# Norm of x in pairs of tiles, the first weight load moved up, and the second column tile three chunks behind in the first projection

## What is computed

```python
mod = einsum('bd,de->be', silu(cvec), w_ada) + b_ada        # 6 vectors of 1024, for two request groups
sh1, sc1, gt1, sh2, sc2, gt2 = split(mod, 6)
h    = rms_norm(x, norm1_g) * (1 + sc1) + sh1
proj = h @ w_in                                             # -> q | k | v | pool input xp | gate a | gate b
pool = multiscale_pool(xp, ...)                             # windows 2/4/8/16 over the tokens
```

## Time and profile before

| | us |
|---|---|
| median of three runs | 1836.32 |
| lowest, highest | 1834.43, 1836.9 |
| the profiled execution | 1835.91 |
| its span | 1834.0 |

### The profile page before, as it was taken

The page is one execution under the profiler, slowest core; times in us unless marked ns, Lnnn a source line. Parts: engine busy times, 40 slices in busy tenths (PEclk is TensorE's granted clock), DMA queues, the critical chain, the costliest instruction groups (busy, mean ns, idle before and its releaser), DMA issues. The chain is left out here.

```text
span 1834.0 us, 22375 instructions
## 1 busy us (share of the span) xinstructions
PE 1615.8 (88%) x8410; PEld 1279.4 (70%) x8410; DVE 905.8 (49%) x1226; ACT 603.4 (33%) x776; POOL 417.8 (23%) x232
## 2 busy tenths in 40 slices
PE   4999999999999699999999899989976599999910
PEld 3778888878887466666666588878865488888810
DVE  5650000006665666667666543331167566666559
ACT  5211121232222444444444500121122255555432
POOL 1111111112222400000000211121135234444353
PEclk9999999999999899999999999999988699999965
DMA  8223434230100600000000232231031378878555
GB/s 346 87 92 135 153 122 151 111 118 23 46 23 15 238 1 0 0 1 1 0 0 0 76 152 91 80 115 60 23 138 79 108 281 276 295 274 291 193 198 180
DMA packets 37888, 209.59 MB, mean 114 GB/s; under 512 B 4304, under 2 KB 5072, under 8 KB 27472
## 3 DMA queue, kind: packets, MB, share of 16 engines
q1 hardware_dynamic: 30352, 181.68, 26.8%
q0 software_dynamic: 7488, 27.27, 4.6%
HBM read 168.03 MB, written 49.28 MB: 118 GB/s over the span
## 5 line engine op out<-in xcount | busy, mean ns | idle before, releaser
L321 PE MATMUL psum<-h_hi,w_hi 128*128 128x512 f32 (+1 forms) x768 | 199.2, 368 | 12.8 <-DVE h_lo L619 7.8
L321 PE MATMUL psum<-h_lo,w_hi 128*128 128x512 f32 (+1 forms) x768 | 193.3, 360 | 0.0
L321 PE MATMUL psum<-h_hi,w_lo 128*128 128x512 f32 (+1 forms) x768 | 192.8, 359 | 0.0
L893 PE MATMUL psum<-probT,vals 128*128 128x512 f32 x384 | 190.9, 593 | 0.0
L954 ACT ACTIVATE prob<-psum,nmax 128x1536 f32<-128x1536 f32 x64 | 98.7, 1542 | 209.1 <-DVE nmax L1032 209.1
L321 PEld LDWEIGHTS psum<-h_hi,w_hi 128*128 128x128 f32 x768 | 128.4, 190 | 42.8 <-issue 22.5
L534 POOL TENSOR_TENSOR w_lo<-w_raw,w_hi 128x1024 fp32r<-128x1024 f32 x32 | 77.2, 2414 | 352.1 <-ACT w_hi L446 352.0
L909 PEld LDWEIGHTS psum<-ident,prob 128*128 128x128 f32 x768 | 92.9, 141 | 78.6 <-issue 72.6
L321 PEld LDWEIGHTS psum<-h_hi,w_lo 128*128 128x128 f32 x768 | 128.5, 189 | 23.0
L1029 DVE TENSOR_REDUCE rmax<-psum 128x1 f32<-128x512 f32 x192 | 128.9, 689 | 31.5 <-PE psum L885 31.4
L321 PEld LDWEIGHTS psum<-h_lo,w_hi 128*128 128x128 f32 x768 | 128.4, 189 | 23.0
(11 more groups left out here) (319 smaller groups left out, 3063.0 us busy)
## 6 DMA issues: line engine op xcount, KB each, us to landing
gu_raw<-in_w_gu SPq DMA_DIRECT2D x16, 2048.0 KB, 10.0
ada<-in_w_ada SPq DMA_DIRECT2D x20, 1024.0 KB, 4.8
w_raw<-in_w_in SPq DMA_DIRECT2D x16, 1024.0 KB, 4.8
dn_raw<-in_w_dn SPq DMA_DIRECT2D x16, 1024.0 KB, 8.3
ybuf<-yst SPq DMA_DIRECT2D x32, 512.0 KB, 7.5
gates<-gst SPq DMA_DIRECT2D x16, 640.0 KB, 3.0
wm_raw<-in_w_merge SPq DMA_DIRECT2D x4, 1536.0 KB, 6.9
xt<-in_x SPq DMA_DIRECT2D x10, 512.0 KB, 7.7
```

The lines of the kernel that those rows point to most:

```text
L321: mm = pe.matmul(psum[:, par_sets[j] + g:par_sets[j] + g + w], a[j][:, k, :], b[:, k, g:g + w], start=(k == 0 and a is w_hi and b is h_hi) ...
L893: mm = pe.matmul(psum[:, PV + 512 * x.par:PV + 512 * x.par + 512], vals[:, x.key0 // P + c, x.kv * HD:(x.kv + 1) * HD], probT[b][g % 2][:] ...
```

## The change

It has six parts.

1. The root and the reciprocals are made for two tiles at a time instead of five. ACT's copies of the transposed tiles stand between its squares (two tiles behind), DVE's stand two tiles behind its scaling.
2. PE turns all ten tiles first and does conditioning blocks 0 and 1 after them, each with its turn at once. In the chunk loop, block k+2 stands ahead of chunk k and its turn behind it, for k below 6. So six blocks and six turns lie in the loop, where four blocks and five turns did.
3. The second column tile runs three chunks behind the first (`LAG`), and its last three chunks follow the loop.
4. DVE modulates two chunks, then makes two `low`, then handles two conditioning blocks.
5. The first `w_raw` is loaded ahead of the conditioning blocks.
6. For the pool input, ACT splits the next weights ahead of its copies to `xpad`, and DVE raises `ada_rows1` and `mods_r1` ahead of the pooling.

```diff
+        LAG = 3
@@ sync
+                sp.dma_start(w_raw[:], io["w_in"][0]).then_inc(s["w_in0"], 16)
                 for i, b in enumerate(FIRST):
                     if i >= 6:
                         sp.wait_ge(s["fa_mm"], i - 5)
                     sp.dma_start(ada_first_buf[i][:], io["w_ada"][b]).then_inc(ada_first[i], 16)
-                    if i == 2:
-                        sp.dma_start(w_raw[:], io["w_in"][0]).then_inc(s["w_in0"], 16)
@@ tensor
-                for t in range(HALF):
+                for t in range(TILES):
                     turn_x(t)
                 pe.wait_ge(s["c_silu"], 1)
-                first_ada(0)
-                turn_x(HALF)
-                first_turn(0)
-                first_ada(1)
...
-                turn_x(HALF + 4)
-                first_ada(3)
+                for i in range(2):
+                    first_ada(i)
+                    first_turn(i)
...
                 for k in range(KC):
+                    if k < 6:
+                        first_ada(k + 2)
                     pe.wait_ge(s["h_hi_r"], k + 1)
                     pe.wait_ge(s["h_lo_r"], k + 1)
                     mm = project_k(0, k)
                     if k == KC - 1:
                         mm.then_inc(s["mm0"], 1)
-                    if k < 4:
-                        first_turn(k + 3)
-                        first_ada(k + 4)
-                    if k == 4:
-                        first_turn(7)
+                    if k < 6:
+                        first_turn(k + 2)
+                    if k >= LAG:
+                        project_k(1, k - LAG)
+                for k in range(KC - LAG, KC):
                     mm = project_k(1, k)
                 mm.then_inc(s["mm1"], 1)
@@ scalar
-                    if t % HALF == HALF - 1:
+                    if t % 2:
                         act.wait_ge(s["x_ss"], t + 1)
-                        h = slice(t + 1 - HALF, t + 1)
+                        h = slice(t - 1, t + 1)
                         nc.scalar.activation(rstd[:, h], ssq[:, h], ACT.Sqrt, bias=eps[:], scale=1.0 / D).then_inc(s["x_sq"], 1)
-                for t in range(TILES):
-                    act_out(t)
+                        if t > 2:
+                            act_out(t - 3)
+                            act_out(t - 2)
+                act_out(TILES - 2)
+                act_out(TILES - 1)
...
                 for n in range(XP_PAIRS):
                     for j in range(2):
+                        split(n + 1, j)
                         act.wait_ge(s[f"mm{j}"], n + 1)
...
                         act.sem_inc(s[f"ps_free{j}"], 1)
-                        split(n + 1, j)
@@ vector
+                for t in range(0, TILES, 2):
+                    h = slice(t, t + 2)
+                    dve.wait_ge(s["x_sq"], t // 2 + 1)
+                    own.step(nc.vector.tensor_scalar(nsq[:, h], ssq[:, h], 1.0 / D, EPS, ALU.mult, ALU.add))
+                    inverse(rstd[:, h], nsq[:, h], ntmp[:, h])
+                    for u in (t, t + 1):
+                        nc.vector.tensor_scalar(xt[:, u, :], xt[:, u, :], rstd[:, u:u + 1], None, ALU.mult).then_inc(s["x_scaled"], 1)
+                        if t:
+                            dve_out(u - 2)
+                dve_out(TILES - 2)
                 dve_out(TILES - 1)
+                for i in range(2):
+                    first_rows(i)
+                    first_mods(i)
...
-                modulate(0)
-                first_rows(3)
-                modulate(1)
-                low(0)
-                first_mods(3)
-                low(1)
-                for k in range(2, KC):
+                for k in range(0, KC, 2):
                     modulate(k)
                     if k < 6:
                         first_rows(k + 2)
+                    modulate(k + 1)
                     low(k)
+                    low(k + 1)
                     if k < 6:
                         first_mods(k + 2)
+                        first_rows(k + 3)
+                        first_mods(k + 3)
...
                 dve.wait_ge(s["h_lo_r"], KC)
+                dve.sem_inc(s["ada_rows1"], 1)
+                dve.sem_inc(s["mods_r1"], 1)
                 for c in range(4):
...
-                dve.sem_inc(s["ada_rows1"], 1)
-                dve.sem_inc(s["mods_r1"], 1)
```

## The result

The changed kernel took 1840.19 us (median of 14 runs, 1837.23 to 1842.25), the one before 1835.76 in the same comparison (14 runs, 1834.4 to 1837.58). The ratio is 1.0022, with a 95% interval of 1.0014 to 1.0029: slower by 4.4 us. The profiled execution took 1839.78 us with a span of 1837.9, 3.9 more than the span before.

What follows compares the result with a forecast made beforehand. TensorE, busy 88%, bounds the kernel; only its idles and low clock in the first 135 us could give. First chunk +2.0, loop +15.8 and pool input -12.3 sum to +5.5, so 1841.4 us; range 1833.5 to 1846.0.

Steps and rivals of the forecast that it cites:

- Part 6 and the gaps: Pool input: TensorE's gaps at 84.24 and 127.52 us close with their slow clock, gaining 5.2 and 7.1, together -12.3 us.
- The norm: Opening stage: all of x turned between 31 and 35.5 us, 33.5 taken; before it was 34.6.
- The first chunk: Start of the chunk loop: first chunk at about 45.3 us against 43.34, +2.0; ends 42.3 and 47.
- The hold by GpSimd: Ahead of the first chunk: POOL's two `w_lo` collide with DVE and hold `modulate(0)` by about 1.5 us.
- The loop: Chunk loop: 46 us with idles plus 7.1 of slow clock, 53.1 against 37.3 before, +15.8; ends +11 and +18.5.
- The ring: Chunk loop: TensorE and DVE wait on each other in turn, leaving TensorE idles of 4.0, 2.2 and 2.9 us.
- The price of the clock: Chunk loop: low clock costs 2.3 us at the start and 1.6 behind each of three idles, 7.1 in all.
- What lies behind 135 us only shifts.: Rest of the kernel after the first 135 us: no change of length, so earlier gains or losses arrive whole.
- A high clock throughout: Rival, chance 0.12: TensorE keeps 2.4 GHz, first chunk at 42.3, loop 46 us; -4.6, 1831.3 us.
- a low clock throughout: Rival, chance 0.08: clock low through the loop's pairs, first chunk at 47, loop near 61 us; +15, 1850.9 us.
- idles without a price: Rival, chance 0.26: the loop's idles are too short for the clock, only the first chunk is slow; +0.7, 1836.6 us.
- a missed turn: Rival, chance 0.12, pool input: the row copy's 0.8 us cover is gone and TensorE stands about 2 us; 1843.4 us.

Runs made afterwards that it cites:

- run 1: The kernel before with part 6 alone: 1825.49 against 1835.61 us, ratio 0.994.
- run 3: The changed kernel with the norm's root made for five tiles again, copies as before: 1838.56 us against 1835.61 for the kernel before, ratio 1.0017.
- the repeats: Both kernels unchanged, profiled once more: one execution each, 1836.72 us (before) and 1836.45 us (changed).
- run 7: Run 6's kernel with DVE making the first low weights instead of POOL, and their load and split earlier: 1816.62 against 1835.71 us for the kernel before.
- run 2: The changed kernel with the old chunk-loop order, no lag, and blocks 0 to 3 ahead of the loop: 1828.66 us against 1835.61 for the kernel before.
- run 4: The changed kernel with a lag of 0 chunks instead of 3: 1843.45 us against 1835.71 for the kernel before, ratio 1.0043.
- run 5: The kernel before with part 6 and the lag of three chunks, conditioning and DVE order as before: 1825.92 against 1835.71 us, ratio 0.9944.
- run 6: The kernel before with part 6, and only the second tile's chunks 6 and 7 behind the first tile's chunk 7: 1820.2 against 1835.71 us.

## Why the prediction was right

Forecast +5.5 us, measured +4.4, inside the range and on the forecast side. The loop's mechanism and its price were right; that the end came so close owes something to luck, as the step on what lies behind 135 us shows. By its steps:

- **Part 6 and the gaps, -12.3.** Measured -12.4 in the profile. Run 1 has -10.1 with one chunk behind the first tile's last where the changed kernel has four. The row copy's cover of 0.8 was 143.72 - 142.44 = 1.3 us. Shown.
- **The norm.** All turned at 35.3, inside 31 to 35.5; the value taken, 33.5, was early, 1.3 of it by the late first square. The ends did not follow from the terms written down (24.5 + 1.2 + 2.2 + 1.1 = 29.0, and 34.9 with the 4.8 and a slow tile). As a step it stayed without effect (run 3).
- **The first chunk, +2.0.** Measured +3.0, and +0.8 between the repeats. The hold by GpSimd came out near its forecast length, 1.1 us for 1.5 (POOL's 36.96 to 41.62 sets it; run 7 takes away the longer one of the kernel before), but on another instruction: the small one with `m`, 1.31 us instead of 0.17. The Trainium skill (GPSIMD Engine Reference, Key points) names contention with VectorE instructions that have two SBUF inputs or run in a two-port mode. The trace agrees that a small scale instruction can be held; in which mode it ran, no row shows. I had also overlooked that TensorE's wait for `w_lo` now stands ahead of block 2, which costs a wait of 1.99 us at 41.98, with no effect, since h comes later.
- **The loop, +15.8.** Measured +16.7. The ring is what the runs show: gone with the old order (run 2), there without the lag (run 4), absent with the lag in the old order (run 5). Mis-sized was the second idle, 3.21 instead of 2.2: the wait of 0.92 at 69.23 is DVE's row copy, which waits for a block that stands behind the lagged chunk. The price of the clock held as a sum: TensorE is busy 43.59 us where the forecast had 46 - 9.1 = 36.9 at full clock, so 6.7 for 7.1. By place, from the rows, it is 1.6 at the start (2.3 was forecast) and 2.1, 1.6 and 1.6 behind the idles (1.6 each). Run 4 shows that it is no fixed price.
- **"What lies behind 135 us only shifts."** This step failed. +7.3 at the turn became +3.9 at the end of the profiled span, and +5.1 became -0.3 in the repeats; 2.0 of the difference each time is the clock in the first units of attention. By the first pair's turn the forecast was 1.8 too low, by the second's 0.4 too high. The medians put it 1.1 too high, with a later stretch that the sum put at nothing and that gave back 3.4 and 5.4 us in the profiles. So part of the closeness is luck.
- **The rivals.** A high clock throughout (the first chunk of the loop was slow, 1.40), a low clock throughout (three matmuls at 0.75 between the idles), idles without a price, and a missed turn all fail by the rows. For the low clock, the Trainium skill (TensorE: Matmul & The Clock Gate, HAM oscillation) has the gate fall back in every turn of a loop of bursts and waits. The trace agrees as to the fall, which came behind each of the three idles; but it was up again 5.4, 5.0 and 4.5 us after each restart (63.94, 77.38 and 90.92), so the loss stayed near 7 us.

## What to carry to other kernels

When work of a strict chain (block, copy, turn, bias) is moved closer to its use, follow the chain through both engines' program orders once around: if engine A's next step waits for something that engine B does only after A's last result, the two take turns, however short each step is. A lag that gives an engine work for a wait at the end takes that work from the waits ahead of it, so it belongs only where the wait is (run 6). And an idle can cost more than its length, by the low clock behind it: in run 1, 4.56 + 1.71 = 6.3 us less idle brought the turn 11.0 us forward.

## What was not expected of the hardware

- A DVE instruction of 128x4 elements was held for 1.1 us beside a GpSimd instruction of two inputs, and ended 0.03 us behind it. In runs 2 and 3 the same one took 1.69 and 1.67 us and ended just behind GpSimd's too.
- Idles of the same length (3.21 us, and 2.22 us) were followed by the full clock in one place and by half of it in another.
- With the same instructions behind the turn, that stretch ranges from 1692.0 to 1697.5 us over eleven profiles, 0.3%, more than half of the effects in question. In the one stretch that was followed it goes with the granted clock. By the end of one profile alone, run 6 lies 1.9 us below run 1; by the medians it is 5.3.
